# Half of each transposed u row's remainder moves from TensorE and ScalarE to VectorE, one expert ahead

## What is computed

```python
q = (xf @ w_pq).reshape(t, PEER_HEADS, 2, PEER_HALF)
s = jnp.einsum('thpd,hpkd->thpk', q, sub_keys).astype(jnp.float32)
sv, si = lax.top_k(s, PEER_TOPK)              # 16 best of 128 keys, per half
comb = (sv[:, :, 0, :, None] + sv[:, :, 1, None, :]).reshape(t, PEER_HEADS, 256)
gv, gp = lax.top_k(comb, PEER_TOPK)           # 16 best pairs -> 128 experts a token
u = expert_u[idx_blk]
a = g_blk * jax.nn.gelu(jnp.einsum('tkd,td->tk', u, x_blk), approximate=False)
out = jnp.einsum('tk,tkd->td', a, expert_v[idx_blk])
```

## Time and profile before

| | us |
|---|---|
| median of 3 runs | 3445.52 (3426.96 to 3452.87) |
| the profiled execution, its own time | 3449.95 |
| its span from first to last instruction | 3448.2 |
| busy: TensorE / VectorE / GpSimd / ScalarE | 3059.4 / 2175.9 / 1469.8 / 1131.8 |
| moved by DMA | 936.06 MB |

### The profile page before, as it was taken

One profiled execution on the slowest core, in us unless ns is written; L12 is line 12 of the kernel. 1 busy time (PEld: TensorE's weight loads), 2 busy tenths in 40 slices (PEclk: granted clock), 3 DMA queues, 4 the chain that ended last, 5 costly groups with the idle time before them and its releaser, 6 DMA issues. The chain is left out here.

```text
span 3448.2 us, 42749 instructions
## 1 busy us (share of the span) xinstructions
PE 3059.4 (89%) x16184; PEld 2384.5 (69%) x16184; DVE 2175.9 (63%) x4561; ACT 1131.8 (33%) x1744; POOL 1469.8 (43%) x1107
## 2 busy tenths in 40 slices
PE   5997879697989989999999999876749999999996
PEld 4885768587778767787777777654437676676665
DVE  4244774415446768887878876588646676655457
ACT  3213551305221133333333333377612222222222
POOL 3100002301210058766767777577724444434432
PEclk9996799899999989999999999999879999999998
DMA  5333012413312199999999999899999999989992
GB/s 180 113 101 122 1 66 88 146 65 101 134 55 74 53 344 408 383 401 357 410 410 409 405 410 411 315 381 415 401 338 358 360 380 379 362 305 375 382 350 107
DMA packets 371628, 936.06 MB, mean 271 GB/s; under 512 B 32848, under 2 KB 134872, under 8 KB 370400
## 3 DMA queue, kind: packets, MB, share of 16 engines
q0 software_dynamic: 147456, 536.94, 39.9%
q1 hardware_dynamic: 223968, 396.39, 32.1%
HBM read 825.53 MB, written 107.67 MB: 271 GB/s over the span
## 5 line engine op out<-in xcount | busy, mean ns | idle before, releaser
L1726 POOL DMA_INDIRECT ex_ring<-in_expert_v,ex_idxT_sb x405 | 471.5, 1164 | 522.2 <-PE ex_ps_v L1751 228.9
L1726 POOL DMA_INDIRECT ex_ring<-in_expert_u,ex_idx_sb x307 | 394.4, 1285 | 185.1 <-issue 87.5
L114 PE MATMUL eo_ps<-eo_v_hi_sb,aT_late_hi 128*128 128x512 f32 x1024 | 411.1, 401 | 42.7 <-DVE aT_late_lo L2361 42.7
L114 PE MATMUL ex_ps_h<-aT_late_hi,ex_uT_hi_sb 128*128 128x512 f32 x1024 | 414.7, 405 | 30.1 <-issue 18.7
L1735 DVE CUSTOM_DVE_ANT_0 ex_ring<-ex_ring,ex_xg 128x1024 f32<-128x1024 f32 x307 | 368.0, 1221 | 92.0 <-DMA ex_ring<-in_expert_u,ex_idx_sb 66.9
L116 PE MATMUL ex_ps_h<-aT_late_hi,ex_uT_lo_sb 128*128 128x512 f32 x1024 | 403.9, 394 | 0.0
L115 PE MATMUL eo_ps<-eo_v_lo_sb,aT_late_hi 128*128 128x512 f32 x1024 | 403.4, 394 | 0.0
L115 PE MATMUL ex_ps_h<-aT_late_lo,ex_uT_hi_sb 128*128 128x512 f32 x1024 | 402.8, 393 | 0.0
L116 PE MATMUL eo_ps<-eo_v_hi_sb,aT_late_lo 128*128 128x512 f32 x1024 | 401.8, 392 | 0.0
L2369 DVE TENSOR_TENSOR eo_acc<-eo_acc,eo_ps 128x1024 f32<-128x1024 f32 x124 | 151.3, 1220 | 284.8 <-PE eo_ps L116 254.4
L1751 PE MATMUL ex_ps_v<-ex_ring,ex_w_sb 128*32 128x512 f32 x1620 | 232.5, 627 | 67.9 <-DMA ex_ring<-in_expert_v,ex_idxT_sb 52.6
(11 more groups left out here) (391 smaller groups left out, 6438.6 us busy)
## 6 DMA issues: line engine op xcount, KB each, us to landing
ex_u_raw<-in_expert_u SPq DMA_DIRECT2D x127, 512.0 KB
eo_v_raw<-in_expert_v SPq DMA_DIRECT2D x124, 512.0 KB
act_d<-ex_act SPq DMA_DIRECT2D x128, 256.0 KB
gate_d<-ex_gate SPq DMA_DIRECT2D x8, 4096.0 KB, 15.6
eo_g_raw<-gate_d SPq DMA_DIRECT2D x64, 512.0 KB
eo_a_raw<-act_d SPq DMA_DIRECT2D x124, 256.0 KB
pin_raw<-in_w_in SPq DMA_DIRECT2D x20, 512.0 KB, 4.5
n_row<-h_d SPq DMA_DIRECT2D x16, 512.0 KB, 5.8
```

The costliest lines, as they stand in the source:

```text
L114: pe.matmul(ps, l_hi, r_hi, start=first, stop=False)
L1726: pool.indirect_dma_start(rows(n), None, table, bass.IndirectOffsetOnAxis(at, 0)).then_inc(ring_in[slot[n]], 16)
```

## The change

VectorE makes columns 512 to 1023 of `uT_lo` directly, as `ps_t` minus `uT_hi`, one instruction for each expert tile. TensorE's `subtract` has one matmul instead of two, and ScalarE's `lo` copies 512 columns instead of 1024. `lower_half(0)` runs before the steps, and `lower_half(e + 1)` at the head of step `e`. The second half of `product(e)` waits for the new semaphore, and `transposes(e)` waits for it as well.

```diff
 def lo(e):
     act.wait_ge(sub_done, e + 1)
-    act.activation(uT_lo[:, e % 2, :, :], ps_t[e % 2][:].rearrange("p (k t) -> p k t", t=P), ACT.Copy).then_inc(uT_lo_done, 1)
+    act.activation(uT_lo[:, e % 2, 0:4, :], ps_t[e % 2][:, 0:HALF].rearrange("p (k t) -> p k t", t=P), ACT.Copy).then_inc(uT_lo_done, 1)
...
+def lower_half(e):
+    dve.wait_ge(uT_hi_done, e + 1)
+    dve.tensor_tensor(uT_lo[:, e % 2, 4:8, :], ps_t[e % 2][:, HALF:D].rearrange("p (k t) -> p k t", t=P),
+                      uT_hi[:, e % 2, 4:8, :], ALU.subtract).then_inc(uT_lo_v_done, 1)
+
+lower_half(0)
 ...
 for e in range(ETILES):
+    if e + 1 < ETILES:
+        lower_half(e + 1)
     count = dots_at(e)
...
     if e >= 2:
         pe.wait_ge(uT_lo_done, e - 1)
+        pe.wait_ge(uT_lo_v_done, e - 1)
...
     pe.wait_ge(uT_hi_done, e + 1)
-    for c in range(2):
-        last = pe.matmul(ps_t[e % 2][:, c * HALF:(c + 1) * HALF], minus[:],
-                         uT_hi[:, e % 2, 4 * c:4 * c + 4, :].rearrange("p k t -> p (k t)"), start=False, stop=True, skip_group_check=True)
-    last.then_inc(sub_done, 1)
+    pe.matmul(ps_t[e % 2][:, 0:HALF], minus[:], uT_hi[:, e % 2, 0:4, :].rearrange("p k t -> p (k t)"),
+              start=False, stop=True, skip_group_check=True).then_inc(sub_done, 1)
...
 def product(e, first, n):
     if first == 0:
         pe.wait_ge(uT_lo_done, e + 1)
+    else:
+        pe.wait_ge(uT_lo_v_done, e + 1)
+    if first == 0:
         if e >= 1:
             pe.wait_ge(gelu_done, e)
```

More of the change, by code:

```diff
@@ L1667, in expert_stages @@
             tr_done, uT_hi_done, sub_done, uT_lo_done = sem("ex_tr"), sem("ex_uT_hi"), sem("ex_sub"), sem("ex_uT_lo")
+            uT_lo_v_done = sem("ex_uT_lo_v")
             minus_done = sem("ex_minus")
```

## The result

| | before | changed |
|---|---|---|
| median, 17 runs each | 3448.58 us | 3464.62 us |
| ratio to before, 95% interval | | 1.0049 (1.0031 to 1.0068) |
| profiled execution, its span | 3448.2 us | 3458.5 us |
| busy: TensorE / VectorE / ScalarE | 3059.4 / 2175.9 / 1131.8 | 3045.3 / 2247.8 / 1077.8 |

The changed kernel is slower by half a per cent, 16 us. A second measurement on another chip gave 1.0043 (1.0023 to 1.0062). That is inside the range of the prediction and within 1%, but on the other side of no change from the 8 us gain that was forecast.

The account below looks back on a forecast made before the run. TensorE's work and the bytes were taken to bound the u stage about equally. The sum -28.8 + 6.4 + 3 + 13.1 - 2 = -8.3 us gave a forecast of 3438 us, range 3414 to 3475.

Parts of the forecast that it names:

- What bounds the kernel: In the u stage, TensorE's own work and the bytes are two limits within a few per cent; VectorE is third.
- The matmul, -28.8: On TensorE's chain in the u stage, 128 removed subtract matmuls of 0.225 us each save 28.8 us.
- the saturated stretch: From 1605 to 2160 us, at 408 GB/s, bytes let only 2.7 of 15.8 us be saved: 13.1 us given back.
- The 22 us of room: By the skill's 425 GB/s, the 1605 to 2160 us stretch has 22 us spare and gives nothing back; not in the sum.
- ScalarE at nothing: Halving `lo` to 512 columns costs or gains nothing, since it runs beside the second half of the product.
- VectorE's instruction: The new 128x512 subtraction takes 0.69 us, 88 us in all, in place of waiting for gathers.
- The late start: At the stage's start the first gather comes 13.4 us later, losing 9.5 us of transfer; net of room, -2 us.
- The bursts: Routing work in steps 10 to 13 and 20 to 23 makes TensorE wait mid-product: 6.4 and 3 us; later tiles nothing.
- The failed step: At step heads VectorE waits for `hi(e + 1)`, with dots and gathers behind it; being held in bursts was taken as nothing.
- the 9 us corridor: VectorE's subtraction must fall after `hi(e + 1)` ends and before the middle of `product(e + 1)`, some 9 us.
- A sign of being wrong that it gave: Corridor wrong if TensorE's waits for VectorE pass 40 us, or GpSimd's dot waits grow and DMA share falls below 1.
- The rival on the other side: VectorE paces through mid-product waits above 28.8 us: 3490 us with all upper bounds, 3467 with half; over 34 us slower: 0.15.

Follow-up runs that it names:

- the start undone and the values' gathers earlier: Changed kernel with experts 0 to 2 made the old way and values' gathers issued one step earlier: 0.9976 and 0.9963 of the kernel before.
- the start-only kernel: Kernel before, with VectorE waiting for hi(e+1) at the heads of steps 0 and 1 only: 1.0008 of the kernel before.
- the wait without the late start: Kernel before, with VectorE waiting for hi(e+1) at the head of each step from step 2 on only: 1.0008 of the kernel before.
- the undone start: Changed kernel with experts 0 to 2 made wholly by TensorE and ScalarE as before: 1.002 and, on a slower chip, 1.0041 of the kernel before.

## Why the prediction was wrong, step by step

- *What bounds the kernel:* right. TensorE and the bytes are two limits of about the same height; fewer bytes alone and one matmul less alone gave next to nothing, both together 0.9908. The 109.5 us of VectorE's gather waits left out 48.3 more that no releaser explains.
- *The matmul, -28.8, with 13.1 given back in the saturated stretch:* the mechanism was right, the size off. Alone it was worth 4.8 us, so 24 are given back: 11 us of the error. The prediction gave back in 555 us of the stage only; that the rest is nearly as tight is likely, but no run separates the stretches. The rate hardly went beyond the 410 GB/s that was counted on: 409 at most over 360 us in the kernel with one matmul less, 412 over 45 us in the changed kernel. The 22 us of room that the prediction weighed for the long stretch never showed: it ran at 397 GB/s in the changed kernel, and at 409 with the start undone and the values' gathers earlier, the highest read over 555 us. One reading was off, too: the granted clock is a mean of two levels, so 0.96 means some 8% of the time at the lower one, and the upper bound of the gain is 31 us and not 30 (an estimate).
- *ScalarE at nothing:* nothing speaks against it. `lo` fell to 599 ns and stayed off the chain.
- *VectorE's instruction:* 0.69 us forecast, 688 ns measured. That its work costs nothing was off by 5 us (1 to 10 by the interval).
- *The late start:* the delay was forecast at 13.4 us and was 13.4. Its net price of -2 us, after filling gaps of the transfers, is within the interval of the start-only kernel (+3, from -4 to +10). On top of the held ring it may be as much as 12, as said above.
- *The bursts:* 9.4 us forecast as waits at the middle of products; 4.0 us by name, and 10.2 us at the routing transposes, which it had not counted. At step 15, for which it had 6.4 us, the waits were 0.95 at the middle of the product and 3.27 at the routing transpose behind it. That the sums are near each other is luck.
- *The failed step:* the price of VectorE's wait at the head of each step. The prediction has it in the sum at -2 us, for the late start alone, and for the bursts of routing, the only other place where it speaks of VectorE being held, it says "I take nothing because gathers land while VectorE is held at the head of a step." They do land, but landed rows are not freed: every dot of the step stands behind the wait for `hi`. VectorE stood 84.5 us for it by name (119.8 with the unexplained), GpSimd waited for dots 119.1 us instead of 35.1, the gathers of values stand in the same order behind those of dots, and TensorE met them late. The wait alone, with no work and nothing taken from TensorE, measured +15 us. The prediction had named who waits behind the wait, and then gave it no price; the 9 us corridor was priced only at its late edge. How the 15 us are made is open: the wait without the late start holds the ring as long and measured 3 us, the late start alone also 3.
- *A sign of being wrong that it gave:* "GpSimd's waits for dots grow so that the DMA share falls below 1" named the place. The waits grew and the rate fell, to 397 GB/s, but the share stayed at 1.01.
- *The rival on the other side* had VectorE as the pacer through the middle of the product. Right in sign; but the middle gave 4 of the 28.8 us that it needed, and the waits lay elsewhere.

The sum with measured terms is -4.8 + 15 + 5 = +15, and 16 was measured. Against the forecast of -8.3 that is 23.5 us of error: 11 in what is given back of the matmul, 7.6 in the ties (15 for the wait, where -2 for the start and 9.4 for the bursts stood), 5 in VectorE's work. Each of these has 3 to 5 us of uncertainty. So the size of the miss has three sources; the turn from a gain to a loss needs the wait, since without its 15 us the measured terms leave nothing.

## What to carry to other kernels

A wait put at the head of an engine's step delays everything that the engine would free in that step. If the engine feeds a ring of transfers, price the slots that it keeps while it stands, and look whose data come later in the same ring. But a long total of such waits is not yet a cost: with 103.7 us of them one kernel here lost 3 us. Where two limits stand at about the same height, taking work from one of them pays only a small part, and a new tie can eat it. Try such a tie at several places of the step, and look at the order of what is fetched: here one reordering of the gathers was worth 27 us on one chip, where the matmul that the change removed had given 5 by itself.

## What was not expected of the hardware

- One subtract matmul of 0.225 us less in each of 128 steps brought 4.8 us; with 31 MB fewer bytes it brought about 37, with 16 to either side, so its own 28.8 is within that.
- In the 8 us window with a 4.06 us wait of TensorE the granted clock was 0.87, in the next 0.91, and 0.79 in the one with the wait of 3.08 us behind it; before the wait a product's matmuls started 0.23 us apart, behind it the first ones 0.43. So a wait can cost more than its length.
- On the slower chips TensorE's waits before a product's first matmuls were 17 to 36 us in all kernels with full loads, and 0.8 to 3.1 us on the faster ones. The gelu has waits there that end with a DMA, or with nothing named (29.1 and 41.8 us in the kernel before), and next to none on the faster ones; that these are for its stores to land is only argued. So is that it may be why the undone start looked better on one kind of chip than on the other.
